# Two-layer hybrid attention and MoE backbone: the twelve small loads of a layer move from GpSimd's queue to SyncE's, and GpSimd's bias rows of layer two to the opening of that layer

## What is computed

```python
def latent_layer(x, cvec, ctx_ak, ctx_av, ctx_bk, ctx_bv, ctx_ckv, ctx_kr, p, rope64, rope32):
    sh1, sc1, g1, sh2, sc2, g2 = modulation(cvec, p['w_ada'], p['b_ada'])
    h = rms_norm(x, p['norm1_g']) * (1 + sc1) + sh1
    qa, ka, va, qb, kb, vb, cq, ckv, kr = split_projection(h @ p['w_in'])
    qa = apply_rope(qa, *rope64)
    ka = apply_rope(ka, *rope64)
    oa = window_attention(qa, repeat_kv(ka), repeat_kv(va), repeat_kv(ctx_ak), repeat_kv(ctx_av), p['a_sink'])
    ob = neighborhood_attention(qb, kb, vb, ctx_bk, ctx_bv, p['b_rpb'])
    qc = mla_query(cq, p)                                   # rms_norm(cq) @ c_w_uq
    k_lat, v_lat = mla_keys(rms_norm(ckv, p['c_kv_norm_g']), kr_rot, p)   # ckv @ c_w_ukv
    k_ctx, v_ctx = mla_keys(ctx_ckv, ctx_kr, p)
    ...
    x = x + g1 * (o @ p['w_out'])
    return ffn_sublayer(x, sh2, sc2, g2, p)                 # router (router_w, router_bias), 6 of 64 experts a token, shared expert
```

## Time and profile before

| | us |
|---|---|
| Median of 3 runs | 1288.08 |
| Lowest and highest | 1286.6, 1289.69 |
| The profiled execution, its own time | 1287.52 |
| Its span, from the first to the last instruction | 1285.6 |
| TensorE busy in the span | 1214.6 (94%) |
| VectorE, ScalarE, GpSimd busy | 310.9, 192.9, 52.1 |
| Bytes moved by DMA | 494.99 MB, 385 GB/s in the mean |

### The profile page before, as it was taken

The page is one execution under the profiler, slowest core; times in us unless marked ns, Lnnn a source line. Parts: engine busy times, 40 slices in busy tenths (PEclk is TensorE's granted clock), DMA queues, the critical chain, the costliest instruction groups (busy, mean ns, idle before and its releaser), DMA issues.

```text
span 1285.6 us, 22837 instructions
## 1 busy us (share of the span) xinstructions
PE 1214.6 (94%) x9511; PEld 800.7 (62%) x9511; DVE 310.9 (24%) x883; ACT 192.9 (15%) x471; POOL 52.1 (4%) x97
## 2 busy tenths in 40 slices
PE   8989999998999999987999999999999999999795
PEld 4435776665667667654544568666557776676463
DVE  2037452123111111110130664321311111111012
ACT  1016221010111111010020351111011011110011
POOL 1330011000000000000020100000000000000000
PEclk9989999999999999998989999999999999999899
DMA  9988989999999999999995895989999999999995
GB/s 365 398 332 355 403 340 360 372 418 421 420 421 420 421 419 422 419 421 420 410 373 199 342 364 198 388 339 420 420 421 420 420 420 420 421 421 421 420 420 198
DMA packets 82117, 494.99 MB, mean 385 GB/s; under 512 B 8908, under 2 KB 13472, under 8 KB 28512
## 3 DMA queue, kind: packets, MB, share of 16 engines
q1 hardware_dynamic: 77984, 484.73, 92.4%
q0 software_dynamic: 3488, 8.29, 2.0%
q10 hardware_dynamic: 544, 0.52, 0.1%
HBM read 491.20 MB, written 2.50 MB: 384 GB/s over the span
## 4 chain that ended last, share of the span: by engine, by line
PE 57%; issue 25%; DMA 8%; DVE 4%; SPq 3%; POOL 1%; ACT 1%; POOLq 0%; ACTq 0%; DVEq 0%
PE ps L1363 14%; PE ps L1306 8%; PE ps L1396 7%; PE ps L1328 6%; PE ps L908 5%; DMA ring<-in_exp_w_down 5%; PE ps L1136 4%; PE ps L875 3%; PE ps L1259 2%; DMA spare<-in_exp_w_up 2%; SPq L603 2%; DMA ring<-in_w_ada 1%; PE ps L1093 1%; SPq L598 1%; PE ps L1118 1%
## 5 line engine op out<-in xcount | busy, mean ns | idle before, releaser
L1363 PE MATMUL ps<-ring,kt_buf 128*32 128x256 f32 (+2 forms) x3008 | 285.0, 384 | 18.3 <-DMA spare<-in_exp_w_up 13.4
L1363 PEld LDWEIGHTS ps<-ring,kt_buf 128*32 128x32 f32 (+2 forms) x3008 | 169.7, 120 | 106.5 <-issue 38.0
L1306 PE MATMUL ps<-kt_buf,attn 128*128 128x128 f32 x1472 | 184.6, 279 | 1.8 <-DVE kt_buf L1994 1.8
L1306 PEld LDWEIGHTS ps<-kt_buf,attn 128*128 128x128 f32 x1472 | 173.7, 193 | 16.9 <-issue 14.3
L1328 PE MATMUL ps<-kt_buf 128*128 128x256 f32 x704 | 163.8, 385 | 3.2 <-DVE kt_buf L2112 1.8
L1396 PE MATMUL ps<-ring,kt_buf 128*32 128x512 f32 (+2 forms) x768 | 158.4, 613 | 8.5 <-DMA ring<-in_exp_w_down 8.5
L1328 PEld LDWEIGHTS ps<-kt_buf 128*128 128x128 f32 x704 | 130.3, 190 | 55.9 <-issue 22.4
L1363 PE MATMUL ps<-spare,kt_buf 128*32 128x256 f32 (+1 forms) x608 | 106.7, 391 | 0.0
L908 PE MATMUL ps<-ring,ht 128*128 128x456 f32 x256 | 99.2, 548 | 0.3 <-DVE ht L1670 0.3
L2100 DVE SCALAR_TENSOR_TENSOR kt_buf<-kt_buf,ps 128x256 f32<-128x256 f32 x44 | 18.5, 421 | 323.1 <-ACT kt_buf L1595 323.1
L1396 PEld LDWEIGHTS ps<-ring,kt_buf 128*32 128x32 f32 (+2 forms) x768 | 42.0, 123 | 67.4 <-issue 64.1
(11 more groups left out here) (313 smaller groups left out, 1108.0 us busy)
## 6 DMA issues: line engine op xcount, KB each, us to landing
ring<-in_exp_w_gate SPq DMA_DIRECT2D x104, 1024.0 KB, 19.5
ring<-in_exp_w_down SPq DMA_DIRECT2D x92, 1024.0 KB, 22.0
ring<-in_exp_w_up SPq DMA_DIRECT2D x84, 1024.0 KB, 19.1
ring<-in_w_ada SPq DMA_DIRECT2D x10, 3072.0 KB, 11.8
spare<-in_exp_w_up SPq DMA_DIRECT2D x22, 1024.0 KB, 26.3
spare<-in_exp_w_gate SPq DMA_DIRECT2D x16, 1024.0 KB, 10.8
attn_w<-in_exp_w_up SPq DMA_DIRECT2D x12, 1024.0 KB, 24.5
ring<-in_w_ada SPq DMA_DIRECT2D x5, 2048.0 KB, 10.6
```

The source lines that it names most:

```text
L1306: last = pe.matmul(ps[:, 4 + b, (c % 4) * P:(c % 4 + 1) * P], h2[:, t, c * P:(c + 1) * P], pick[:, t, :], start=(t == 0), stop=(t == NG - 1))
L1363: last = pe.matmul(ps[w * e:w * (e + 1), b, 0:DE], xg[:, k, w * e:w * (e + 1)], half_of(chunk_of(l, load_of(part, i, e)))[:, k, :], start= ...
```

## The change

The eight loads of `attention_loads` and the four of `small_loads` become one function in SyncE's block. In layer one SyncE issues them behind the second `w_ada` piece. In layer two it issues them behind the third `w_in` piece, after a wait for the last experts of layer one that used the chunks `attn` and `attn_w`. GpSimd keeps the bias rows and the bias table. Those of layer two are now written at the opening of layer two, behind the power of the mean squares (L758), and no longer in the expert part of layer one.

```diff
+            def small_loads(l):
+                for dst, src in ((w_uq, I["c_w_uq"][l].rearrange("(k p) n -> p k n", p=P)),
+                                 (w_ukv, I["c_w_ukv"][l]),
+                                 (cache_ak, I["cache_a_k"][0, l].rearrange("t h d -> t (h d)")),
+                                 (cache_av, I["cache_a_v"][0, l].rearrange("t h d -> t (h d)")),
+                                 (cache_bk, I["cache_b_k"][0, l].rearrange("t h d -> t (h d)")),
+                                 (cache_bv, I["cache_b_v"][0, l].rearrange("t h d -> t (h d)")),
+                                 (cache_ckv, I["cache_c_kv"][0, l]),
+                                 (cache_kr, I["cache_c_krope"][0, l]),
+                                 (w_router[:], I["router_w"][l].rearrange("(k p) n -> p k n", p=P)),
+                                 (rbias[:], I["router_bias"][l:l + 1, :].to_broadcast([P, E])),
+                                 (kvg[:], I["c_kv_norm_g"][l:l + 1, :].to_broadcast([P, CKV])),
+                                 (sink[:, 0:8]..., I["a_sink"]...)):
+                    sp.dma_start(dst, src).then_inc(s_small, 16)
...
+                    if l == 0 and es[i - NSLOT] == ("opening", 3):
+                        sp.wait_ge(s_set, 6)
+                        small_loads(l)
+                    if l and i == NSLOT - 1:
+                        for c in (ATTN_C, ATTN_W_C):
+                            part_b, step_b, _ = LOADS[LAST[c]]
+                            sp.wait_ge(S[used_by[part_b]], done - (STEPS - 1 - step_b))
+                            settle()
+                        small_loads(l)
...
         def _(pool):
-            def small_loads(l):
...
-            def attention_loads(l):
...
                     pool.wait_ge(S["half_mm"], 4)
                     pool.wait_ge(s_skew, 16)
-                    bias_table(0)
-                    small_loads(0)
-
-                attention_loads(l)
+                bias_table(l)
                 pool.wait_ge(s_skew, 16 + 16 * 12 * (l + 1))
...
                 pool.tensor_tensor(rs[:], ms[:], mhalf[:, 0:NG], ALU.pow).then_inc(S["rs"], 1)
-                if l + 1 < DEPTH:
-                    pool.wait_ge(S["key"], l + 1)
-                    small_loads(l + 1)
-                    bias_table(l + 1)
```

More of the change, by code:

```diff
@@ L548, in settle @@
                 sp.sem_inc(s_sp, 1)
+            def small_loads(l):
[10 more added lines that the diff above has]
+                                 (kvg[:], I["c_kv_norm_g"][l:l + 1, :].to_broadcast([P, CKV])),
+                                 (sink[:, 0:8].rearrange("p (j a) -> p j a", j=2)[:, :, 0:A_GROUP],
+                                  I["a_sink"][l:l + 1, :].rearrange("o (j a) -> o j a", j=2)
+                                  .to_broadcast([P, 2, A_GROUP]))):
+                    sp.dma_start(dst, src).then_inc(s_small, 16)
+            used_by = {"gate": "gl", "up": "gu", "down": "y1"}
             done = 0
@@ L605, in load_half @@
                                  ).then_inc(there, 16)
-                used_by = {"gate": "gl", "up": "gu", "down": "y1"}
                 def attention_done():
```

## The result

| | before | after |
|---|---|---|
| Median (lowest to highest), 6 runs each | 1288.21 (1285.62 to 1289.69) | 1282.17 (1279.09 to 1283.59) |
| The profiled execution's own time | 1287.52 | 1283.38 |
| Its span | 1285.6 | 1281.5 |
| GpSimd busy | 52.1 | 37.6 |

The ratio is 0.9953, with a 95% interval of 0.9937 to 0.9968: the changed kernel is faster by 6.0 us in the medians, and by 4.1 us in the two profiled executions. Predicted were 7.4 us. The time lies in the range; the question that is left is why 1.4 to 3.3 us of the forecast are missing. The six runs of the changed kernel are three of 1279.1 to 1281.0 and three of 1283.4 to 1283.6, and the profiled one is of the upper three: the trace shows where 3.3 us are missing, in one execution.

What follows compares the result with a forecast made beforehand. Layer one's opening was taken as bound by twelve small loads behind GpSimd's stalled issue; 6.01 us earlier start plus 1.36 us faster matmuls gave 7.4, so 1288.08 - 7.4 = 1280.7 us, range 1278.5 to 1285.5 (8 in 10).

Steps and rivals of the forecast that it cites:

- the pattern: Layer two's opening, with no small-load wait, as model for layer one: L875 starts 6.01 us earlier, its matmuls save 1.36.
- 2.3 + 3.4 = 5.8. They land at 71.3: Layer one's small loads on SyncE's queue: 2.3 us for long rows, 3.4 for short, after the `w_ada` piece lands at 65.5.
- lower bound: Layer one's small loads by bytes alone: 1.78 MB at 419 GB/s, 4.2 us, landing at 69.7.
- upper bound: Layer one's small loads at 53 ns a short row: landing at 75.5, 2.3 us lost, 1.4 more if the clock falls.
- late landing: Rival, layer one's opening: short rows cost 53 ns or more, `sink` lands at 75 or later, 1283 to 1286; chance 0.10.
- hidden costs: Layer two's later small loads, `w_in` pieces and bias rows: each lateness covered by other work, so nothing lost.
- worst case 690: Layer two's opening: GpSimd free of the bias chain by 690 us, ahead of the power wanted at 709.6.
- slower: Rival, layer two: the bias chain holds GpSimd past 709.6 us, delaying the power, VectorE and TensorE; 1290 to 1292, chance 0.06.
- Absorbed: Rival: weight stream bound by bytes from the attention part on, earlier slots only deepen the queue; 1286 to 1288, chance 0.10.
- no sooner: Rival, layer one's opening: landing hangs on the 16 engines, the twelve still land at 79; 1288 us, chance 0.04.
- signs that were named: Layer one: `sink` before 73.2, no VectorE wait, L1001 at 75.3, clock 1.00, L1021 near 82.5, L1306 near 177.5, end near 643.9.
- if L1306 keeps less than 6 us of the gain: Sign against the forecast at layer one's first expert step, which was to move from 184.87 to near 177.5.

Runs made afterwards that it cites:

- e1: The changed kernel in layer one only, layer two as in the kernel before (small loads and bias rows on GpSimd): 1281.78 us, ratio 0.9946 to the kernel before.
- e2: The change in layer two only; in layer one all twelve small loads stay on GpSimd's queue behind the bias rows: 1287.32 us, ratio 0.9996 to the kernel before.
- e3: The changed kernel with the load of `sink` moved from last to first of the twelve: 1279.41 us, ratio 0.9933 to the kernel before.
- e4: The changed kernel with `w_router` and `rbias` back on GpSimd's queue, behind the bias table's reads, own semaphore: 1279.51 us, ratio 0.9935 to the kernel before.
- e5: The changed kernel with both edits, `sink` first and `w_router` and `rbias` on GpSimd's queue: 1278.55 us, ratio 0.9927 to the kernel before.
- e9: The changed kernel with half of the router's weights (512 of 1024 rows) on GpSimd's queue: 1279.3 us, beside 1286.28 for the kernel before, one run each.
- e10: The changed kernel with the router's weights on SyncE's queue in two transfers instead of one: 1283.64 us, beside 1286.28 for the kernel before, one run each.
- e6: The changed kernel with two unread matmuls in TensorE's gap ahead of L1001 in layer one: 1280.39 us, ratio 0.9944 to the kernel before.
- e7: The changed kernel with layer one's small loads behind the third `w_ada` piece instead of the second: 1294.84 us, ratio 1.0055 to the kernel before.
- e8: The kernel before with layer one's twelve small loads ahead of the bias rows on GpSimd's queue, nothing moved to SyncE: 1290.09 us, ratio 1.0015.

## Why the prediction was right, and where it was off

**The mechanism and the place.** The forecast put all of the gain into the opening of layer one, by the end of the wait for the twelve small loads. It is so: e1 has all of it, e2 none.

**What is late next.** The forecast took layer two's opening as the pattern: from L908's end to L1021, 1.48 + 5.56 = 7.04 us. Where the loads were in time it was 81.27 - 74.50 = 6.8 us (e3; the same in e4, e5 and e9), the 48 matmuls taking 5.36 us. The pattern was right, and 7.4 us was what the change would have given with that landing: e3 is 8.4 us shorter than before in its span, 0.9 of it because L908 ended that much sooner in that execution (74.50 against 75.44).

**The mis-sized term: "2.3 + 3.4 = 5.8. They land at 71.3".** They landed at 74.8, inside the bounds (69.7 to 75.5) but near the upper one. The failed step is that I made the landing of the last load a matter of the 16 engines' rate alone. For the loads ahead of it this was right: the `w_ada` piece landed at 66.5 (51.10 + 15.4, forecast 65.5), and `kvg`, the last but one, 5.5 us behind it at 72.0, where the sum had 5.8. The rows agree with the 24 ns that were taken: from 68 to 70 us 1384 packets, 1163 of them under 512 B, took a share of 0.948, which is 22 ns of one engine each (0.948 x 32 / 1384). What was missing is how the last one comes to land: SyncE is held by outstanding rows until 68.5 (e9, e10), so that the last load is issued at 69.07, and this one then takes 5.7 us, with the engines at 0.30. The prediction saw that "an issue is held", and asked what it does to the next `w_ada` piece, but not to the last small load itself: it had the twelve issued by 56, and they took until 69.5. (One unit is mixed in the lower bound: the twelve loads are 1.82 MB, not 1.78, which moves 4.2 us to 4.3 and changes nothing.)

**What it cost.** Against the pattern L1021 came at 10.1 us after L908's end (85.60 - 75.50) in place of 6.8: 3.3 us. Of these 1.7 us are the clock (7.05 - 5.36, given back in e6), and 1.5 to 1.6 the later start (TensorE's gap of 1.53). The prediction's upper bound had exactly this pair in it, 2.3 and 1.4 us, and its rival *late landing* told the mechanism; the case that came lies between the forecast and this rival, in its time nearer to the forecast.

**The hidden costs were hidden.** The next `w_ada` piece went at 69.55, against 69.34 in the earlier trace rows, and no engine waited for it. The bias table in layer one was in time. In layer two the last small load landed at 675.3, GpSimd was free at 669.3 (worst case 690), TensorE went from the end of L908 to L875 in the 1.48 us of before, and neither VectorE nor TensorE waits for a small load, for the last `w_in` pieces or for the power. The rival *slower* had put the danger there; the way to a slower kernel is elsewhere, in the place of the loads in SyncE's list (e7) or in GpSimd's queue (e8).

**The shift reaches the end.** What follows L1021 in layer one takes the same time in every kernel to within 3 us, whatever came before:

| | L1021 starts | span | difference |
|---|---|---|---|
| before | 89.78 | 1285.6 | 1195.8 |
| after | 85.60 | 1281.5 | 1195.9 |
| e1 | 84.02 | 1281.0 | 1197.0 |
| e2 | 89.32 | 1284.3 | 1195.0 |
| e3 | 81.27 | 1277.2 | 1195.9 |
| e4 | 81.96 | 1277.4 | 1195.4 |
| e5 | 83.21 | 1277.2 | 1194.0 |
| e6 | 83.99 | 1278.6 | 1194.6 |
| e7 | 96.02 | 1292.0 | 1196.0 |
| e8 | 94.16 | 1290.9 | 1196.7 |

Over a start that moves by 14.8 us the difference moves by 3.0, and without a trend. (An effect of 1 or 2 us can therefore be read at L1021 and not from one span: e1 starts L1021 1.6 us before the changed kernel and ends 0.5 us before it.) *Absorbed* is refuted by this, and *no sooner* by the landing at 74.8. In the changed kernel the window 183 to 228, which is the earlier trace rows's 190 to 235 moved by the forecast's 7 us, has the same 45.00 us of TensorE and share 0.92.

**The signs that were named.** Of those in layer one's opening none was met in the changed kernel: `sink` landed at 74.78 and not before 73.2, L1001 started at 77.03 and not 75.3, the clock from 80 to 85 was 0.75 and not 1.00, and L1021 started at 85.60 and not 82.5. In e3, where every load was down by 71.96, all four were met: `sink` landed at 65.6, L1001 started at 74.39, the clock was 1.00 and L1021 started at 81.27. Further on in the changed kernel:

```profile
180.70 3.07 PE L1306 MATMUL ps<-kt_buf,attn 128*128 128x128 f32 x16 [0.96 <-DVE kt_buf L1994]
647.71 1.99 PE L1328 MATMUL ps<-kt_buf 128*128 128x256 f32 x8 [0.71 <-ACT kt_buf L1606]
```

L1306 started 4.2 us sooner (184.87 before) and the last of layer one 3.5 us sooner (651.2 before), where the forecast had 7.4. The prediction had named "if L1306 keeps less than 6 us of the gain" as a sign that it is wrong, and by this execution it came; `sink` at 74.78 missed another, 75, by 0.2 us. What it pointed at is not a gain that is lost on the way, since 4.2 us is all that L1021 had: it is the late `sink` again. So the time lies in the range although one part of the forecast's mechanism, loads that are all down in time, did not come about in this execution.

**The rule of the Trainium skill.** The Trainium skill (DMA: Bandwidth & Descriptors, Issuing engines are not separate DMA queues) has the choice of the issuing engine save sequencer time only, which it calls usually small. The trace agrees that it is time of issue that was saved, and not that this is small here: 6.0 us in the medians. But SyncE's queue isn't the quicker one. The twelve loads took it 17.55 us from the first issue to the last (51.52 to 69.07), and GpSimd 15.51 (57.09 to 72.60). The last one landed 4.25 us sooner because the first was issued 5.57 us sooner, clear of the bias rows and the 8.59 us of hold behind them; 2.04 of that went to the slower issuing, and 0.72 came back in the landing of the last (5.71 against 6.43 us).

**What stays open.** What sets the length of each hold: the outstanding rows of the large pieces ahead count (0.98 us at `krope` in e7, 6.1 to 7.5 in the six others that have it in the eighth place on this queue), but how many rows the queue takes no run shows. Why 256 rows of 12 bytes take 5.7 us with the engines at a share of 0.30. And why the runs of one kernel spread by 2 us and more to either side (the 17 of the kernel before in one series go from 1284.95 to 1290.1, which is 0.4% and more than the 0.2% given at the start): in the profiles the end of L908 moves by up to 2.2 us from execution to execution, and no run shows how much of the spread that is.

## What to carry to other kernels

When a wait stands for several loads on one semaphore, find which lands last and why: its issue behind held ones, or its own time from issue to landing, can be the bound while the DMA engines are idle. Put the one that is slowest to land first, and the ones needed late on another queue or behind another semaphore. And price a short gap on TensorE with what it does to the clock of the work behind it.

## What the runs showed of the hardware

- The holds of SyncE's issue went with the rows still outstanding, and not with the number of transfers or the bytes: halving the 1024 rows of one transfer took the hold behind it from 4.91 to 2.20 us (e9); splitting them into two transfers left the sum at 5.8 us (e10). It was held with 0.4 MB left to move, and not held with over 4 MB. One profile each.
- A transfer of 3 KB in 256 rows of 12 bytes took 5.7 us to land (5.3 to 5.7 in e1, e6, e7, e9 and e10 too), one of 64 KB in 128 rows of 512 bytes 3.4 us, both issued within 0.5 us of each other on one queue. Behind a 3 MB piece the same 3 KB took 15.1 us (e3).
- Full share, fewer bytes: 1.01 at 298 GB/s while 1910 of 2186 packets were under 2 KB, against 1.01 at 419 in the expert part. With few short packets it was once 1.01 at 279 as well (60 to 65 us), for a reason that isn't known.
- TensorE's granted clock after a gap of 0.44 us stayed 1.00 (2.4 GHz). With a gap of 1.53 us it was 0.90 in the window of 5 us that holds it and 0.75 in the next; after 5.84 us it was 0.50 (1.2 GHz) in the window from 80 to 85. A stretch of 5.36 us then took 7.05 and 6.92. In e2, e7, e8 and e10, with gaps of 5.96, 11.88, 8.42 and 1.48 us, it took 6.86, 7.03, 7.45 and 7.02: a gap of 1.5 us cost this stretch as much as one of 12. With the gap of 1.53 us filled by matmuls the clock was 1.00 again (e6).
- GpSimd's queue held its issue for 15.42 us behind six transfers (e8), and for 7.43 us at the router's load behind the reads of the bias table (e4, hidden there).
